# Attention tiles of a hybrid decoder layer: two k-steps of the key and value product moved ahead of the scores, transposed keys moved to another bank

## The reference

```python
xn = rmsnorm(x, norm_w)
q, k, v, g_attn, u, g_ssm = split(xn @ w_in)
q = rope(rmsnorm(q per head, q_norm_w)); k = rope(rmsnorm(k per head, k_norm_w))
s = q @ k.T / sqrt(64)           # 128-query blocks, keys of this block and the one before
p = softmax([s masked to a window of 128, sink])[..., :-1]
o = p @ v
a = rmsnorm(o * silu(g_attn))
```

## Time and profile before

| | us |
|---|---|
| median of 3 runs | 1780.39 (1779.35 to 1783.53) |
| the profiled execution | 1779.05 |
| its span, first to last instruction | 1777.3 |
| PE busy in the span | 1687.8 |
| DVE busy | 1186.7 |
| ACT busy | 623.4 |
| POOL busy | 344.8 |

### The profile page before, as it was taken

The page is one execution under the profiler, slowest core; times in us unless marked ns, Lnnn a source line. Parts: engine busy times, 40 slices in busy tenths (PEclk is TensorE's granted clock), DMA queues, the critical chain, the costliest instruction groups (busy, mean ns, idle before and its releaser), DMA issues. The chain is left out here.

```text
span 1777.3 us, 24711 instructions
## 1 busy us (share of the span) xinstructions
PE 1687.8 (95%) x8604; PEld 1346.2 (76%) x8604; DVE 1186.7 (67%) x2652; ACT 623.4 (35%) x1631; POOL 344.8 (19%) x425
## 2 busy tenths in 40 slices
PE   6899999999999999799999999788979999999999
PEld 5677777787777777588888888555667888888886
DVE  7787888767878788585634334799765656456532
ACT  5445455444445543422111111245341222222200
POOL 2122222212222222100014442022111111111110
PEclk9899999989999999899999999899989999999999
DMA  6311111213322110335635618476673445635222
GB/s 234 118 63 63 63 63 63 79 50 122 106 83 74 51 40 13 109 81 105 122 89 109 138 62 138 150 224 204 174 146 129 132 102 135 157 122 137 92 92 68
DMA packets 197420, 191.16 MB, mean 108 GB/s; under 512 B 118064, under 2 KB 153520, under 8 KB 197296
## 3 DMA queue, kind: packets, MB, share of 16 engines
q1 hardware_dynamic: 191360, 184.83, 37.9%
q10 hardware_dynamic: 5936, 4.75, 0.9%
HBM read 131.81 MB, written 57.73 MB: 107 GB/s over the span
## 5 line engine op out<-in xcount | busy, mean ns | idle before, releaser
L1165 PE MATMUL ps_b<-b_WH,b_XH 128*128 128x512 f32 (+1 forms) x776 | 285.6, 368 | 0.7 <-issue 0.4
L1167 PE MATMUL ps_b<-b_WH,b_XL 128*128 128x512 f32 (+1 forms) x776 | 276.4, 356 | 0.0
L1166 PE MATMUL ps_b<-b_WL,b_XH 128*128 128x512 f32 (+1 forms) x776 | 275.9, 356 | 0.0
L1165 PEld LDWEIGHTS ps_b<-b_WH,b_XH 128*128 128x128 f32 x776 | 147.3, 190 | 28.6 <-issue 8.8
L1167 PEld LDWEIGHTS ps_b<-b_WH,b_XL 128*128 128x128 f32 x776 | 147.2, 190 | 21.6
L1166 PEld LDWEIGHTS ps_b<-b_WL,b_XH 128*128 128x128 f32 x776 | 147.7, 190 | 18.6
L1120 POOL TENSOR_TENSOR b_XL<-b_XT,b_XH 128x1024 fp32r<-128x1024 f32 x33 | 80.7, 2444 | 377.2 <-ACT b_XH L1364 315.2
L1430 ACT ACTIVATE b_SM<-ps_b,b_small 128x128 f32<-128x128 f32 x256 | 113.7, 454 | 111.8 <-DVE b_small L1613 109.2
L795 PE MATMUL ps_g<-w_X0H,w_nextH 128*128 128x464 f32 x320 | 122.1, 382 | 2.7 <-DVEq L847 2.6
L797 PE MATMUL ps_g<-w_X0H,w_nextL 128*128 128x464 f32 x320 | 119.7, 374 | 0.0
L796 PE MATMUL ps_g<-w_X0L,w_nextH 128*128 128x464 f32 x320 | 119.4, 373 | 0.0
(11 more groups left out here) (339 smaller groups left out, 3765.0 us busy)
## 6 DMA issues: line engine op xcount, KB each, us to landing
b_XT<-in_xb SPq DMA_DIRECT2D x33, 512.0 KB, 4.1
b_XR<-in_x SPq DMA_DIRECT2D x33, 512.0 KB, 4.6
w_XT<-in_xt SPq DMA_DIRECT2D x36, 464.0 KB, 4.3
l_X<-in_xr SPq DMA_DIRECT2D x32, 512.0 KB, 4.5
out_out<-l_OUT SPq DMA_DIRECT2D x32, 512.0 KB, 3.0
scr_gs<-e_TG SPq DMA_DIRECT2D x36, 232.0 KB, 2.0
scr_u<-w_ST SPq DMA_DIRECT2D x12, 696.0 KB, 13.2
g_U<-scr_u SPq DMA_DIRECT2D x64, 130.5 KB
```

The source lines that it names most:

```text
L1165: pe.matmul(bank[:, 0:c1 - c0], XH[b][:, k, :], WH[:, k, c0:c1], start=(k == 0), stop=False)
L1166: pe.matmul(bank[:, 0:c1 - c0], XH[b][:, k, :], WL[:, k, c0:c1], start=False, stop=False)
L1167: mm = pe.matmul(bank[:, 0:c1 - c0], XL[b][:, k, :], WH[:, k, c0:c1], start=False, stop=(k == KD - 1))
```

## The change

On TensorE the first two k-steps (6 matmuls) of the key and value product of tile t+2 are issued after the gate transposes of tile t+1 and before the scores of t+1; the remaining six k-steps stay where the whole product was. This holds for t = 0 to 30, so before the scores of tiles 1 to 31. Since this product writes bank 1 while the transposed keys are still being read, `KTB` moves to bank 7, columns 0 to 127, one of the score banks. The product's wait changes from the copy of the transposed keys to the low part of x and to the copies of keys and values of the tile before; the key transpose waits for the copy of the transposed keys before it.

```diff
-        KTB, SUMB, OB = ps[:, 1, 256:384], ps[:, 2, 0:2], ps[:, 4, :]
+        KTB, SUMB, OB = ps[:, 7, 0:P], ps[:, 2, 0:2], ps[:, 4, :]
...
-        LAST, BEHIND = NT - 1, 3
+        LAST, BEHIND, BEFORE = NT - 1, 3, 2
...
-                def project_kv(t):
-                    if t:
-                        pe.wait_ge(kT_out, t)
-                    project(t, ZKV, DA, DA + 2 * P, kv_full)
+                def project_kv(t, part=range(KD)):
+                    if 0 in part:
+                        pe.wait_ge(x_lo, t + 1)
+                        pe.wait_ge(k_out, t)
+                        pe.wait_ge(v_out, t)
+                    project(t, ZKV, DA, DA + 2 * P, kv_full, part)
...
                 def k_transpose(t):
                     chain.wait(pe, tile(t))
-                    pe.wait_ge(k_out, t + 1)
-                    pe.wait_ge(v_out, t + 1)
+                    if t:
+                        pe.wait_ge(kT_out, t)
                     pe.transpose(KTB, RK[:], ID[:]).then_inc(kT_full, 1)
...
-                        project_kv(t + 1)
+                        project_kv(t + 1, range(BEFORE if t else 0, KD))
...
                             gate_transposes(t + 1)
+                            project_kv(t + 2, range(BEFORE))
```

## The result

The changed kernel takes 1794.04 us (median of 4 runs, 1793.34 to 1797.42) against 1781.96 (4 runs, 1779.35 to 1784.72): ratio 1.0068, 95% interval 1.0049 to 1.0088, so 12.1 us slower. The forecast was 1794.0.

What follows compares the result with a forecast made beforehand. The prediction took DVE's loop, 20.48 us per ordinary tile, as the bound, with PE close behind. Terms of +5.2 and blocked adds of +8.4 made +13.6, so 1794.0 us, range 1781.5 to 1798.5.

Steps and rivals of the forecast that it cites:

- What bounds the kernel: DVE's loop sums to the whole 20.48 us tile, so scores delayed after the gate lengthen it unless given back.
- The insertion: On PE between gate end and scores: six matmuls take 0.80; 0.86 becomes 1.38, +0.52 in an ordinary tile.
- What is given back: DVE's small instructions after the reduce: XL 0.72 earlier disturbs them less, -0.33, leaving an ordinary tile +0.19.
- The blocked adds: DVE's last rotary add in tiles 8, 20, 24, 28 waits behind POOL's XL: +2.1 each, +8.4 together.
- The sum: Whole kernel: +5.2 of drift and other terms plus +8.4 of blocked adds, together +13.6 us, giving 1794.0.
- A: Rival, late tiles: XL reaches the lock while the add holds it, so no flip; 1785.6 us, chance 0.18.
- B: Rival: PE is the bound, its 0.28 gap before the scores is filled; 1772.9 us, chance 0.12.
- C: Rival: drift, and blocked adds in more tiles (4, 12, 16) or longer; 1800 us, chance 0.06.
- D: Rival: nothing that counts; waiting elsewhere refills the gap, or tile 15 balances the drift; 1781 us, chance 0.09.
- The wait for the key copy: DVE's four waits, 2.0 us in all, go; less insertion, with the other sample tiles, +0.3 in sum.
- Tile 15's clock: Granted clock in tile 15, averaging 0.84: effect taken as 0, with -4 to +2 us as bounds.

Runs made afterwards that it cites:

- e3: Kernel before, no k-step moved, ACT copying XH ahead of the values so that XL starts earlier: 1788.62 us, ratio 1.0054.
- e8: Kernel before with XH made ahead of the key copy and POOL's XL waiting for the key rotation, no k-step moved: 1771.49 us, ratio 0.9949.
- e7: Changed kernel with one k-step moved, XH made ahead of the key copy, XL waiting for the key rotation: 1769.81 us, ratio 0.9941.
- e1: Changed kernel with POOL's XL waiting until DVE has finished the key rotation: 1779.98 us, ratio 1.0003.
- e2: Kernel before with POOL's XL waiting until DVE has finished the key rotation: 1776.21 us, ratio 0.9979.
- the repeat: Changed kernel run and traced again with no edit, to check the clock: one run, 1793.47 us.

## Why the prediction was right, step by step

*What bounds the kernel.* "Whatever delays the scores after the gate, and is not given back inside DVE's row of work, lengthens the tile": right for the changed kernel. For the kernel before it was half of the truth. Two loops closed within 0.1 us of each other there: PE's at 20.46, and DVE's at about 20.38, an estimate from the earlier trace rows with 0.75 from gate to scores, as in the late tiles, in place of 0.86. The forecast read the 0.86 as DVE's alone, though it had itself named the keys, on PE's line, as what the scores wait for. e3 and e8 show that less time on DVE alone does not shorten a tile, e7 that relief of both does.

*The insertion.* 1.38 forecast, 1.35 measured, by two errors that cancel: the first moved matmul came 0.41 after the transposes' start, not 0.52, and the six with the change back to the scores took 0.89, not 0.80.

*What is given back.* I left 0.1 for tables touching L88; they do not (reduce to the end of RK 3.73, as undisturbed). So ordinary tiles lose 0.10, not 0.19 (which put them at 20.57, just under the 20.6 to 20.8 that were to show it), and those behind a late one do too, where 0.31 was forecast. Taken over the stage, this term was mis-sized: +5.2 us forecast for all but the blocked adds, where e1 against e2 gives 3.5. And one term is missing: tile 2 is 1.4 shorter, its old blocked add being gone, and tile 1 0.5. I had shown tile 2's add as the model for the late tiles, and not asked what the change does to it. In the repeat, whose clock stayed at full from tile 3 on but for tiles 15 and 31, S32 is 9.8 later than before and the four late tiles are 8.7 of it, which leaves +1.1 for all the rest.

*The blocked adds.* +2.1 each forecast, +2.17 measured, in the four tiles named; XL forecast 0.20 earlier against DVE, measured 0.23 (9.84 after the maxima began, was 10.07). XL starts 0.16 after the third rotary instruction and takes 2.40, so it was not held up, which fits the 0.15 that I had taken from XL's 0.10 wait in the earlier trace rows. e1 takes the mechanism away and e3 makes it without the change: this is shown, and at 8.7 us it is the larger part of the loss. The margins were thin: tile 16 escaped it by 0.13.

*The sum.* 13.6 forecast, 12.1 between the medians. That the time itself agrees to 0.1 us is luck: the median of the kernel before stood at 1780.39 in the forecast and at 1781.96 in the result. In the traces 9.8 to 12.6 lie in the attention tiles. The rest of the first trace's 18.3 is in stages that the change does not touch: from the first matmul of the early projections to the end it is 1039.2 in the kernel before, 1044.7 in the changed one, 1043.4 in its repeat, and between 1039.5 and 1045.0 in the other traces whatever the kernel. So that the total came within 1.5 us of the forecast is in part luck: +5.2 stood where the repeat has +1.1 at S32, and the difference stood in for things that I had not counted: sometimes the clock behind a blocked tile, and a late part of the program that in the trace of before is the shortest of all twelve. The range held all of it.

*Rivals.* A (order does not flip) falls on the trace. B (PE is the bound, gap filled) is wrong for this change and right for e7, where its condition, half a microsecond of slack on DVE, was made. C did not come; D falls with the measured time. The wait for the key copy went, as forecast. Tile 15's clock moved its length within 30.4 and 32.0 over all traces, inside the bounds given.

## What to carry to other kernels

When an edit moves work by tenths of a microsecond, look at what its consumers' consumers start beside: here an element-wise instruction on POOL changed places with one on DVE, three engines away from the edit, and cost more than the edit was worth. Check the margin of such neighbours before, and fix the order with a wait if it is small. A gap on one engine can be filled up to the point where the next loop closes and no further; work out both loops' lengths before choosing how much to move.

## What the runs showed of the hardware that was not expected

A DVE instruction of 128x128 elements takes 2.2 us longer when it starts 0.07 us after a POOL instruction of 2.41 (e3), and loses nothing by starting 0.05 before it; the profile shows the wait as its length. One of 128x10 waits in the same way (L88 in tile 9 of the kernel before, 1.85 in place of 0.23). POOL gets through as soon as about 0.15 us after such a 128x128 instruction's recorded start, well before its recorded end (0.28 to 0.30); this is worked out from XL's length: starting 0.05 behind the add it is 0.10 longer (2.51), 0.13 behind it, in tile 16 of the changed kernel, 0.02 longer (2.43), and 0.16 behind it not at all (2.40). The Trainium skill (SBUF — State Buffer, "Who interferes with whom") has the block last the whole instruction of the one that came first; for POOL's instruction the traces agree, for DVE's recorded length they do not.
